# Four stage changes of a two-block transformer kernel: tiles read before the last products, sixteen square buffers, first pairs crossed by halves, token sums over 272 columns

## What is computed

```python
# first block
h = rmsnorm(x, g_mix) * (1 + sc1) + sh1
x = x + (1 + gt1) * mixer(h, ...)              # ends with "merged @ w_o"
h = rmsnorm(x, g_ffn) * (1 + sc2) + sh2
x = x + (1 + gt2) * conv_ffn(h, w_up, conv_w, conv_b, w_down)
x = rmsnorm(x, g_final)
# second block, 16 meta tokens ahead of the 256
h = concat([meta, x])
z = rmsnorm(h, g_pre_mix) @ w_in
mix = concat([y_conv, y_rwkv]) @ w_out
h = h + rmsnorm(mix, g_post_mix)
f = conv_glu(rmsnorm(h, g_pre_ffn), w_gate_up, conv_ffn, w_down)
h = h + rmsnorm(f, g_post_ffn)                 # the last 256 tokens are the output
# rmsnorm(x, g) = x * rsqrt(mean(x * x over the 2048 features) + 1e-6) * g
```

## Time and profile before

| quantity | value |
|---|---|
| device time, median of 3 runs | 3277.89 us (3274.33 to 3282.74) |
| the profiled execution's own time | 3289.89 us |
| span from its first to its last instruction | 3288.2 us |
| PE busy | 2976.5 us, 91% of the span |
| DVE busy | 2052.7 us, 62% |
| ACT busy | 1349.4 us, 41% |
| mean granted TensorE clock | 0.946 of 2.4 GHz |
| chain of work that ended last | PE 76%, DVE 12%, DMA 7%, issue 3%, ACT 2% |

### The profile page before, as it was taken

The page is one execution under the profiler, slowest core; times in us unless marked ns, Lnnn a source line. Parts: engine busy times, 40 slices in busy tenths (PEclk is TensorE's granted clock), DMA queues, the critical chain, the costliest instruction groups (busy, mean ns, idle before and its releaser), DMA issues.

```text
span 3288.2 us, 62097 instructions
## 1 busy us (share of the span) xinstructions
PE 2976.5 (91%) x24776; PEld 2827.5 (86%) x24776; DVE 2052.7 (62%) x2899; ACT 1349.4 (41%) x1893; POOL 167.4 (5%) x288
## 2 busy tenths in 40 slices
PE   2698699799998999998999999979798999999997
PEld 1698698799997888887999999978688999998996
DVE  7874868677746666665445555755556666665445
ACT  1353333333335555554435344313344444443433
POOL 0121012122200000000000000011000000000000
PEclk6797899899999999999999999989898999999998
DMA  9775367688854555554544446500252555554552
GB/s 356 277 251 171 103 196 242 203 281 294 268 186 133 190 183 190 190 183 155 190 180 166 140 141 186 170 15 4 78 167 93 189 179 188 182 184 163 190 180 88
DMA packets 407396, 585.36 MB, mean 178 GB/s; under 512 B 20385, under 2 KB 368673, under 8 KB 389857
## 3 DMA queue, kind: packets, MB, share of 16 engines
q1 hardware_dynamic: 384720, 516.24, 47.2%
q0 software_dynamic: 20480, 67.13, 6.0%
q10 hardware_dynamic: 2064, 0.13, 0.0%
HBM read 581.35 MB, written 2.10 MB: 177 GB/s over the span
## 4 chain that ended last, share of the span: by engine, by line
PE 76%; DVE 12%; DMA 7%; issue 3%; ACT 2%; DVEq 0%; POOL 0%; POOLq 0%; SPq 0%; ACTq 0%
PE bank L437 16%; PE bank L438 16%; PE bank L439 16%; PE bank L444 15%; PE bank L445 8%; DMA late_ring<-w_ada_dram 5%; PE bank L1138 3%; DVE wlo L379 3%; DVE work L1942 1%; DMA ring<-w_ada_dram 1%; DVE work L1911 1%; PE bank L703 1%; ACT whi L368 1%; DMA ring<-w_in_dram 0%; DVE mats L2429 0%
## 5 line engine op out<-in xcount | busy, mean ns | idle before, releaser
L379 DVE TENSOR_TENSOR wlo<-ring,whi 128x1024 fp32r<-128x1024 f32 x908 | 1084.6, 1220 | 544.2 <-ACT whi L368 542.7
L368 ACT ACTIVATE whi<-ring 128x1024 fp32r<-128x1024 f32 x908 | 942.4, 1053 | 1058.7 <-PE bank L439 702.0
L437 PE MATMUL bank<-hx,whi 128*128 128x256 f32 (+2 forms) x2704 | 783.9, 290 | 62.7 <-DVEq L562 19.7
L439 PE MATMUL bank<-hx,wlo 128*128 128x256 f32 (+2 forms) x2704 | 775.4, 287 | 0.0
L438 PE MATMUL bank<-hx,whi 128*128 128x256 f32 (+2 forms) x2704 | 775.0, 287 | 0.0
L444 PE MATMUL bank<-hx,whi 128*128 128x512 f32 x2112 | 744.6, 396 | 7.4 <-DVE hx L750 7.4
L445 PE MATMUL bank<-hx,wlo 128*128 128x256 f32 x2112 | 593.4, 281 | 0.0
L437 PEld LDWEIGHTS bank<-hx,whi 128*128 128x128 f32 x2704 | 518.9, 192 | 72.0 <-DVEq L562 20.1
L437 PE MATMUL bank<-xs,whi 128*128 128x256 f32 (+1 forms) x1920 | 545.3, 284 | 38.2 <-DVE xs L430 37.6
L439 PE MATMUL bank<-xs,wlo 128*128 128x256 f32 (+1 forms) x1920 | 544.6, 284 | 0.0
L438 PE MATMUL bank<-xs,whi 128*128 128x256 f32 (+1 forms) x1920 | 544.0, 283 | 0.0
(11 more groups left out here) (320 smaller groups left out, 2713.6 us busy)
## 6 DMA issues: line engine op xcount, KB each, us to landing
ring<-w_in_dram SPq DMA_DIRECT2D x136, 1024.0 KB, 5.4
ring<-w_up_dram SPq DMA_DIRECT2D x88, 1024.0 KB, 5.1
ring<-w_down_dram SPq DMA_DIRECT2D x88, 1024.0 KB, 4.8
ring<-w_gate_up_dram SPq DMA_DIRECT2D x88, 1024.0 KB, 5.1
late_ring<-w_ada_dram POOLq DMA_DIRECT2D x256, 256.0 KB, 4.0
ring<-w_ada_dram SPq DMA_DIRECT2D x32, 1024.0 KB, 7.5
ring<-w_o_dram SPq DMA_DIRECT2D x16, 1024.0 KB, 4.8
ring<-w_out_dram SPq DMA_DIRECT2D x16, 1024.0 KB, 5.2
```

Of the source, the lines that this page charges most:

```text
L368: nc.scalar.activation(half_of(whi, u, h, n), ring[:, u % PLAN[phase][3], h * n // 2:(h + 1) * n // 2], ACT.Copy)\
L379: nc.vector.tensor_tensor(half_of(wlo, u, h, n), ring[:, u % PLAN[phase][3], h * n // 2:(h + 1) * n // 2], half_of(whi, u, h, n).bitcast(F ...
L437: nc.tensor.matmul(out_ap, a[0], b[0], start=start, stop=False, **kw)
L439: return nc.tensor.matmul(out_ap, a[1], b[0], start=False, stop=stop, **kw)
```

## The change

It touches each place where a stage ends with a norm, and two more.

1. In wo, down and down2 DVE waits only for the first half of the last unit before it reads tiles 0 to 7 (`first_half_read`), and for the second half before tiles 8 to 15. Of the next stage's unit 1 only the first half is rounded ahead; its second half comes behind the root (wo, mix2) or in the middle of the hand-over (down).
2. Squares have 16 buffers (in the upper half of hx). The table of the root is loaded by a small operation before the squares (`load_root_table`). In mix2 the squares of tiles 0 to 7 are formed and added (three DVE additions, 4, 2 and 1 tiles wide) beside the last iteration, so that nine products are left. In down2 ACT squares straight from PSUM.
3. In the first iteration of up, rkv and up2 (`CROSSED`), the units come in the order pair 0 first half, pair 1 first half, pair 0 second half, pair 1 second half. In the first pair PE waits tile by tile, not quarter by quarter. ACT and DVE first split units 2 to 5 and then read out pairs 0 and 1.
4. `token_sums` sums all 272 columns with a stationary matrix of ones, 16 plain products, and in rkv 16 more of 256 columns with the squared gains; they stand behind the third unit. `token_spread`, the diagonals and their copies are gone; root and reciprocal are taken over [128, 272].
5. The last norm scales during the copy out of PSUM and then multiplies and adds four tiles at a time.
6. `keep_warm` issues plain 256-column products whose results nobody reads: 10 before and 10 behind the end of phase 1, 40 at the end of phase 4, 12 behind each of the sums after wo and mix2.

```diff
+CROSSED = ("up", "rkv", "up2")
+def pair_of(phase, u, i):
+    if phase in CROSSED and first(i) and u < 4:
+        return u % 2, u // 2
+    return u // 2, u % 2
...
-        sq = sb("sq", [P, 2, NT], at=xs_at)
+        sq = sb("sq", [P, KD, NT], at=hx_at + 4 * KD * NT)
...
+        def first_half_read(eng, phase):
+            eng.wait_ge(used, twice(phase, PLAN[phase][2] - 1, PLAN[phase][1] - 1) + 1)
...
+        def norm_pe(pe, n, free=None, free_squares=1, added=False):
+            if free:
+                pe.wait_ge(*free)
+            made = squares_made["pe"]
+            squares_made["pe"] += KD
+            ks = [0] + list(range(KD // 2, KD)) if added else list(range(KD))
+            for k in ks:
+                pe.wait_ge(squared, made + max(KD // 2 + 1 if added else free_squares, k + 1))
+                last = nc.tensor.matmul(bank[:, 0, 0:n], ones[:], sq[:, k, 0:n], start=k == 0, stop=k == KD - 1)
+            last.then_inc(summed, 1)
...
+            def keep_warm(b, count):
+                for _ in range(count):
+                    nc.tensor.matmul(bank[:, b, 0:T], ones[:], consts[:, 0:T], start=True, stop=True)
...
+            keep_warm(2, 10)
             phase_end(pe, 1)
+            keep_warm(2, 10)
             phase_end(pe, 2, meet=False)
...
+            pe.wait_ge(relu_done, 9)
+            keep_warm(0, 40)
             phase_end(pe, 4)
...
+                    last = nc.tensor.matmul(bank[:, 6, 0:NT], ones[:], tok_squares[:, k, :], start=k == 0, stop=k == KD - 1)
+                if n == 1:
+                    for k in range(KD):
+                        last = nc.tensor.matmul(bank[:, 7, 0:T], gf_squared[:, k:k + 1].to_broadcast([P, P]), tok_squares[:, k, META:NT],
+                                                start=k == 0, stop=k == KD - 1)
...
+                    if first(i):
+                        for u in range(4):
+                            s, half = pair_of(phase, u, i)
+                            for quarter in (2 * half, 2 * half + 1):
+                                quarter_of_pair(phase, s, u, quarter, i, *src(s)[0:2], bank_free, src(s)[2])
+                            if u == 2 and sums:
+                                token_sums(sums)
...
             norm_pe(pe, T, free=(tile_done, TOLD["wo"] + 2))
+            keep_warm(1, 12)
...
+            load_root_table()
+            square_tiles(T, range(KD), lambda k: x1[:, k, :], lambda k: act.wait_ge(tile_done, TOLD["wo"] + k + 1))
+            norm_root(act, T)
+            round_half("up", 1, 0, 1)
...
+                    crossed = phase in CROSSED and first(i)
+                    if crossed:
+                        for u in range(2, 5):
+                            rest_unit(phase, u, i)
+                        if inverses:
+                            token_inverses(inverses)
+                        rest_unit(phase, 5, i)
+                        read(0, i)
+                        read(1, i)
...
+                    if last and u == 5:
+                        dve.wait_ge(squared, 2 * KD + KW)
+                        for n in (4, 2, 1):
+                            step(nc.vector.tensor_tensor(sq[:, 0:n, :], sq[:, 0:n, :], sq[:, n:2 * n, :], ALU.add))
...
+                if n < 4:
+                    q = slice(4 * n, 4 * n + 4)
+                    last = nc.vector.tensor_tensor(fT[:, q, 0:T], fT[:, q, 0:T], factor, ALU.mult)
+                if n:
+                    q = slice(4 * n - 4, 4 * n)
+                    nc.vector.tensor_tensor(x1[:, q, :], x1[:, q, :], fT[:, q, 0:T], ALU.add).then_inc(tile_done, 4)
```

More of the change, by code:

```diff
@@ L681, in build @@
         norms = {"act": 0, "pe": 0, "dve": 0}
[L682 to L692 removed]
+        squares_made = {"act": 0, "pe": 0}
@@ L885, in _, with quarter_of_pair, product @@
                 last.then_inc(used, 1)
+            def quarter_of_pair(phase, s, u, quarter, i, rhs, width, free, wide=False):
+                half = quarter // 2
+                is_split(pe, phase, u, quarter % 2, i)
+                w = parts(u, KH, UNIT)
+                by_tile = phase in CROSSED and first(i) and s == 0
+                def product(t, k):
+                    q = 2 * s + t
+                    a, start, stop = [x[:, k, t * P:(t + 1) * P] for x in w], half == 0 and k == 0, half == 1 and k == KH - 1
+                    x = rhs[:, half * KH + k]
+                    if wide:
+                        return twofold(q, a, x, start, stop)
+                    return threefold(bank[:, q, 0:width], a, [x[:, 0, :], x[:, 1, :]], start, stop)
+                if quarter == 0:
+                    for t in range(2 if by_tile else 1):
+                        free(2 * s + t)
+                if by_tile:
+                    for k in halves(quarter):
+                        tile_handed(half * KH + k)
+                        for t in range(2):
+                            last = product(t, k)
+                else:
+                    for t in range(2):
+                        if quarter == 0 and t:
+                            free(2 * s + 1)
+                        for k in halves(quarter):
+                            last = product(t, k)
+                last.then_inc(used, 1)
@@ L906, in pair_of_tiles @@
-                    last.then_inc(used, 1)
+                    quarter_of_pair(phase, s, 2 * s + quarter // 2, quarter, i, rhs, width, free, wide)
                     if between:
@@ L1827, in mix @@
                     round_unit("mix2", u, i)
+                    if last and u == 4:
+                        square_tiles(NT, range(KW), lambda k: mixT[:, k, :], lambda k: act.wait_ge(evac["mix2"], k + 1))
                 if last:
-                    ahead(round_unit, "mix2", i, last)
+                    round_unit("up2", 0, 0)
+                    round_half("up2", 1, 0, 0)
                 else:
@@ L2161, in body @@
                     step.begin(i)
-                    for s in range(per // 2):
+                    crossed = phase in CROSSED and first(i)
+                    if crossed:
+                        for u in range(2, 5):
+                            rest_unit(phase, u, i)
+                        if inverses:
+                            token_inverses(inverses)
+                        rest_unit(phase, 5, i)
+                        read(0, i)
+                        read(1, i)
+                    for s in range(2 if crossed else 0, per // 2):
                         if s < per // 2 - 1:
```

296 lines of the change are left out of this document (130 added, 166 removed).

## The result

The changed kernel takes 3240.32 us as the median of four runs (3238.01 to 3245.81), the kernel before 3280.31 beside it (3274.33 to 3285.64). The ratio is 0.9878 with a 95% interval of 0.9866 to 0.9889: 40 us less, where 45 were forecast from the profile and 3233 us from the median. The profiled execution took 3239.63 us, its span is 3237.9, PE is busy for 2978.7 us of it (92%; 2976.5 before), and the mean granted clock is 0.961 instead of 0.946. The profiled spans are 50.3 us apart, 10 more than the medians, because the profiled execution of the kernel before lay 9.6 us above its median and this one does not.

The account below looks back on a forecast made before the run. Time was to be won where PE stands still or runs at the lower clock, in six places: 6.3 - 2.0 - 9.5 - 9.8 - 21.0 - 9.0 = -45.0 us, from the median 3277.9 to 3233 us. Range 3221 to 3247.

Parts of the forecast that it names:

- the six places: Hand-over before sb, pick of 64, wo to up, down to rkv, mix2 to up2, tail: together -45.0 us.
- mix2 to up2: From mix2 through up2: earlier copies, nine products instead of sixteen, earlier reciprocal, shorter token sums; -21.0 us.
- Before sb: End of phase 1: first ten spare products delay the meeting and DVE's reciprocal, nothing covers it; +6.3 us.
- Pick of 64: End of phase 4: forty spare products delay nothing and let dsa start at full clock; -2.0 us.
- wo to up: From wo through up: earlier adds, reciprocal 7.7 us earlier, PE following DVE tile by tile; -9.5 us.
- down to rkv: From down through rkv: PE goes straight on, one more unit before token sums that leave the clock high; -9.8 us.
- (b): Clock falls in the hand-over, costing 2 to 3 us in up and up2, one in rkv: 3239; 8%.
- Tail: Behind down2: earlier copies, sums without two-buffer ping-pong, eight wide operations instead of 32; -9.0 us.
- (a): Low parts come late behind read-outs and inverses in up, rkv, up2; 2 to 3 us each: 3241; 13%.
- (c): Start is free: sb's own waits for late loads might absorb the 6.3 us: 3227; 9%.
- (d): Slower: plain products with ones don't lift the clock, everything made of them doubles, +78 us: 3311; 3%.
- (e): Eight tiles can't be read early, DVE still splitting halves; adds start 2.8 us later at four places: 3244; 4%.

Follow-up runs that it names:

- the early split: Changed kernel, with both halves of unit 2 rounded and split inside the hand-overs to up, rkv and up2: 3235.64 us, 0.9851.
- the ones in sb: 14 and 5 spare products in sb's last step, added to the kernel with the early split and without the first ten: 3231.28 us, 0.9839.
- the late read: Changed kernel, but in wo, down and down2 DVE again waits for the last unit's second half before reading the first tile: 3250.67 us, 0.9891.

## Why the prediction was right, step by step

The forecast of -45.0 us stands against -43.9 in the stretches that it named and -40 in the medians. The forecast time (3277.9 - 45.0 = 3232.9 us) was 7.4 us too low: 2.4 because the median of the kernel before came out at 3280.3 with the later executions, 1.1 in the six places, 3.9 in stretches outside them. That the six places together are only 1.1 off is partly luck: the start and the pick of 64 missed by 0.8 and 0.9 in one direction, mix2 to up2 by 2.1 in the other. By its own steps:

- **Before sb, +6.3.** Measured 5.3 to 6.6 over eight profiles with the ten against six without. Right, with the mechanism: the meeting stands behind PE's drain, and sb does not cover it. In absolute time the reciprocal stood at 116.79, not at 119.5, since the loads came earlier and the true cost was a little smaller.
- **Pick of 64, -2.0.** Worth 2.5 us. I took 2.0 of a possible 2.6 because dsa "then waits for other things". It does wait, 4.50 us for a split at 447.65 (4.34 without the forty), but that wait moves along with the start, so nearly the full value of the cold start is had up to there.
- **wo to up, -9.5.** 9.65. The adds start 2.8 us ahead of wo's last product instead of 2.3 behind it, the reciprocal ends 9.7 us behind it (9.6 forecast), the first product shown in the trace is 12.9 behind it (12.5), unit 2 begins at 26.3 (26.0), with a wait of 1.06 (1.2).
- **down to rkv, -9.8.** 9.43. First product 0.5 us behind down's last (0.3), wait 1.28 (1.2), sums 14.2 (14.3). The next 2.9 us are given back at conv2's start: PE waits 2.55 us instead of 1.06 there, in a wait for loads that the change leaves as it was, and the 144 products behind it take 1.4 us longer, as the clock is at half for 3.1 us of them. Over the profiles the wait is 1.1 to 2.7 us long, and how long it is for the kernel before in other executions than the profiled one stays open.
- **mix2 to up2, -21.0.** 18.9: the term that was mis-sized. The reciprocal ended 8.3 us behind mix2's last product, not 7.6, so the first product came 0.8 late, and unit 2 took 7.4 us instead of 5.8, as the clock fell behind PE's wait of 1.84 us. All five profiles with that wait of 1.84 us have the fall behind it; the eight others (wait gone, or 0.49 us) do not, and took 531.9 to 535.0 us for all of up2. This is not rival (b), which had the clock fall in the first units. That fall came too: not at up or in rkv of the changed kernel, but in up2, and there in ten of the thirteen profiles somewhere in the hand-over. It cost nothing, since DVE sets the start of unit 2. The larger part of the gain is as forecast: the reciprocal ends 8.3 us behind mix2's last product instead of 16.8, and the token sums take 7.1 us instead of 15.8.
- **Tail, -9.0.** 8.6 to the last addition; the last transfer then ends 0.4 us later relative to it. The prediction's sentence that the clock is at 0.50 around each gap does not hold here: in the kernel before it was 1.00 until 3271.5, past the sums. No term rests on it.

Of the rivals, (a) did not come: behind unit 2 PE waits for no low part in the first iteration of up, rkv and up2. (b) is answered above. (c), the free start, is refuted at its place. (d) is refuted: sums at clock 1.00. (e) is refuted, and its price was wrong too: 4.8 us for the three places that read early instead of 2.8 at each of four, because behind wo and down2 PE's sums hide much of it.

Where I had a number right without the reason, the experiments say so. I had let the twelve spare products through as "hidden", and before the run without them expected a loss; they are worth nothing. The schedule with crossing gave the right ends, but the schedule without it gives the same ends at up and rkv and a better one at up2, so the right ends are no evidence that crossing helps; the prediction did not ask what the old order would give with PE waiting tile by tile. By the rows, the gain at wo comes from sums without the ping-pong of two buffers (7.1 us instead of 11.0, begun 3.0 us earlier against wo's last product) and from PE that follows tile by tile; no run isolates these. What bounds a hand-over then is DVE, up to the split of unit 2, and this the early split shows.

The error that matters is in none of these steps. I took all stretches that the change does not touch as fixed. The longest of them, from sb to qi, took 176.2 to 177.7 us in five profiles with the first ten spare products, 181.1 to 185.1 in three more, and 182.4 to 185.0 in four without them and without the ones in sb. So its scatter is larger than what the first ten cost. Whether the shift of the start causes the long case, or chance does, is not settled: two kernels with the same work up to that point (the changed one and the one with the late read) took 176.8 and 185.1, so chance alone can make the difference. In medians, leaving out the ten brought 0.9 us in one pair of kernels and 5.0 in the other.

## What to carry to other kernels

When a hand-over from a slow engine to a fast one is long, ask what the fast engine wants next behind it, and put that inside the hand-over; making the fast engine's own work cheaper or warmer there changes only how long it waits. Test a combined edit part by part: here the order of PE's units would have got the credit for an order on DVE and ACT, and a counterpart run that kept the one and undid the other took one edit. And measure the stretches that an edit does not touch in a few profiles before a difference of medians is explained, since one of them moved by 9 us here.

## What the runs showed of the hardware

- The clock fell under a PE that was busy without a gap. In ki, where products of 16 columns (0.11 us from one to the next) alternate with products of 256, the granted clock fell from 1.00 to 0.50 at some point between 303 and 321 us in every profile, and even when it had been held at 1.00 until ki's start. The Trainium skill ("TensorE: Matmul & The Clock Gate", Part 1) says that the point at which the clock rises under steady work varies between runs, by about 0.5 us. The falls here vary too, and by more: 314 and 321 us in two kernels with the same work up to there (the late read and the early split).
- Plain products that nobody reads held the clock at 1.00 for as long as they lasted (forty of them in 17.5 us). Behind the one-column sums, which run at half clock, the clock rose under them: in the kernel without the first ten, the ten that are left took 7.2 us (110.4 to 117.6), their records fell from 0.43 us apart to 0.22 at 115.8, and sb's products had records of 0.28 us from the second on.
- A wait of 1.84 us of PE, at the end of up2's hand-over, was followed by 3.4 us at half clock in all five profiles that have it; with the wait at 0.49 us or gone there was no fall at this place. The waits of 1.06 us at up and 1.28 in rkv were followed by none.
- With the root's table loaded ahead, DVE's reciprocal starts 0.55 us behind the last sum at wo, 1.14 before, when the load of 1.28 us was partly in the way. The Trainium skill ("ScalarE: Activation LUTs", What ACT_TABLE_LOAD costs) has 2.66 us for load and drain together; no row here shows more than the 1.28: in the kernel before the last square ends at 1021.36, the load runs from 1021.38 to 1022.66, and the root starts at 1022.67.
